# A third pair of PSUM banks after three norms, level chains on other slots, and 37 low parts on VectorE instead of GpSimd, in a two-block transformer kernel

## What is computed

```python
# block 1
h = rms_norm(x, mix_pre_g);  q, k, v, f, qh, i, g = split(h @ w_in)
o_da = differential_attention(q, k, v)      # 8 heads, causal softmax
o_hg = hgrn2(f, qh, i, g)                   # 8 heads, decayed linear attention:
#   attn[t,s] = sum_c q[t,c] k[s,c] exp(b[t,c] - b[s,c]),  b = cumsum(log f)
x = x + rms_norm(concat(o_da, o_hg) @ w_out)
h = rms_norm(x, cross_pre_g);  qx = h @ w_cq;  kx, vx = split(rms_norm(mem) @ w_ckv)
x = x + rms_norm(softmax(qx kx^T) vx @ w_co)
x = x + rms_norm((silu(gate) * up) @ w_ffn_out)      # hidden width 5632
# block 2
h = rms_norm(x);  p, q, k, v, g_lr, r, gates = split(h @ w_in_2)
# pooling branch, gated linear attention with the same kind of decay, gates, w_out_2, second FFN
```

## Time and profile before

| what | value |
|---|---|
| median of 3 runs | 2911.67 us |
| the profiled execution | 2912.26 us, of which the span is 2910.4 us |
| PE busy | 2847.8 us, 98% of the span |
| DVE busy | 1753.1 us, 60% |
| ACT busy | 1397.6 us, 48% |
| POOL busy | 194.7 us, 7% |
| granted TensorE clock, mean | 0.993 of full speed |

### The profile page before, as it was taken

The page is one execution under the profiler, slowest core; times in us unless marked ns, Lnnn a source line. Parts: engine busy times, 40 slices in busy tenths (PEclk is TensorE's granted clock), DMA queues, the critical chain, the costliest instruction groups (busy, mean ns, idle before and its releaser), DMA issues.

```text
span 2910.4 us, 37252 instructions
## 1 busy us (share of the span) xinstructions
PE 2847.8 (98%) x15236; PEld 2431.7 (84%) x15236; DVE 1753.1 (60%) x1936; ACT 1397.6 (48%) x1705; POOL 194.7 (7%) x109
## 2 busy tenths in 40 slices
PE   8998999999999999999999999999999999999998
PEld 6887888778888888887788887888878888888886
DVE  5668765666645555556468654666566654565555
ACT  5555444564444443445545544454454444443443
POOL 1022210110000000002222000000010000000001
PEclk9999999999999999999999999999999999999999
DMA  7554445455665656555555465665656566556654
GB/s 245 160 159 151 118 157 189 160 166 182 196 196 179 195 181 202 179 185 166 162 166 167 145 189 165 186 191 187 195 175 194 182 198 191 182 178 205 186 183 159
DMA packets 432090, 520.56 MB, mean 179 GB/s; under 512 B 18032, under 2 KB 346144, under 8 KB 431280
## 3 DMA queue, kind: packets, MB, share of 16 engines
q1 hardware_dynamic: 430304, 510.52, 56.6%
q0 software_dynamic: 1328, 7.42, 0.7%
q10 hardware_dynamic: 288, 0.24, 0.1%
HBM read 516.01 MB, written 2.11 MB: 178 GB/s over the span
## 4 chain that ended last, share of the span: by engine, by line
PE 89%; DVE 5%; DMA 2%; ACT 2%; issue 1%; POOL 0%; SPq 0%; DVEq 0%; ACTq 0%
PE PS L460 88%; DVE RL L1366 1%; DVE AR L1366 1%; DMA RAW<-in_w_in 1%; DVE X L1372 1%; ACT RH L923 1%; DMA RAW<-in_w_ffn_out 1%; DMA RAW<-in_w_ffn_down 1%; PE PS L463 1%; ACT SP L923 1%; DVE A_HL L1372 0%; ACT AR L923 0%; POOL ST L1970 0%; DVE AR L1369 0%; POOL RL L1947 0%
## 5 line engine op out<-in xcount | busy, mean ns | idle before, releaser
L1366 DVE TENSOR_TENSOR RL<-RAW,RH 128x1024 fp32r<-128x1024 f32 x917 | 1126.2, 1240 | 899.8 <-ACT RH L923 895.6
L923 ACT ACTIVATE RH<-RAW 128x1024 fp32r<-128x1024 f32 (+1 forms) x961 | 1004.1, 1057 | 1003.7 <-PE PS L460 616.0
L460 PE MATMUL PS<-A_HL,RH 128*128 128x512 f32 (+1 forms) x3280 | 1165.5, 399 | 8.7 <-DVE AR L1366 3.2
L460 PE MATMUL PS<-A_HL,RL 128*128 128x256 f32 (+1 forms) x3280 | 920.7, 281 | 0.0
L460 PEld LDWEIGHTS PS<-A_HL,RH 128*128 128x128 f32 (+1 forms) x3280 | 616.4, 188 | 159.0 <-issue 4.7
L460 PE MATMUL PS<-B_HL,RH 128*128 128x512 f32 x1856 | 656.6, 399 | 0.5 <-DVE B_HL L1372 0.5
L460 PEld LDWEIGHTS PS<-A_HL,RL 128*128 128x128 f32 (+1 forms) x3280 | 620.2, 189 | 1.4 <-issue 0.7
L460 PE MATMUL PS<-RH,A_HL 128*128 128x512 f32 x1728 | 539.1, 391 | 0.1
L460 PE MATMUL PS<-B_HL,RL 128*128 128x256 f32 x1856 | 520.8, 281 | 0.0
L460 PEld LDWEIGHTS PS<-B_HL,RH 128*128 128x128 f32 x1856 | 348.7, 188 | 87.1 <-DVE B_HL L1372 0.7
L460 PEld LDWEIGHTS PS<-RH,A_HL 128*128 128x128 f32 x1728 | 325.1, 188 | 69.0 <-DVE RL L1366 1.0
(11 more groups left out here) (105 smaller groups left out, 1069.4 us busy)
## 6 DMA issues: line engine op xcount, KB each, us to landing
RAW<-in_w_in SPq DMA_DIRECT2D x288, 512.0 KB, 3.8
RAW<-in_w_ffn_in SPq DMA_DIRECT2D x176, 512.0 KB, 4.5
RAW<-in_w_ffn_out SPq DMA_DIRECT2D x88, 512.0 KB, 4.7
RAW<-in_w_ffn_gate SPq DMA_DIRECT2D x88, 512.0 KB, 4.5
RAW<-in_w_ffn_up SPq DMA_DIRECT2D x88, 512.0 KB, 4.5
RAW<-in_w_ffn_down SPq DMA_DIRECT2D x88, 512.0 KB, 4.7
RAW<-in_w_out SPq DMA_DIRECT2D x64, 512.0 KB, 4.6
RAW<-in_w_branch_b SPq DMA_DIRECT2D x32, 512.0 KB, 4.4
```

What stands on the lines that cost most here:

```text
L460: return g.matmul(o, l, r, start=start, stop=stop, skip_group_check=True)
L923: return g.activation(o, i, f, bias=bias, scale=scale, accum_out=accum)
L1366: return g.tensor_tensor(o, a, b, f)
```

## The change

Six things change. (1) Three passes, the first pass of k0, ckv1, and LR, go to the pair [4, 5] (`THIRD`) instead of taking the next of the two pairs; they are the passes that follow a normed group. Every later pass outside the FFNs' own rotation shifts with that, and cross attention moves to the banks 6, 7 and the pair of cq's first pass (`CROSS_BANKS`). (2) The 37 low parts of the set `shared` (every third slot of f, qh, i, g0, g1, K, Q, P) are made by VectorE; 7 stay on GpSimd. (3) Chains 0 and 2 start 2 slots later against chains 1 and 3, and chains 2 and 3 half a slot later as a whole. (4) `DA_NORM` moves from slots 75 and 80 to 88 and 91. (5) A head's product with the values, and the copy behind it, come half a slot later. (6) The steps of cross attention come half a slot later, with the one on VectorE at +3 moved to +3.5 and those on TensorE and ScalarE at +4.5 moved to +5.

```diff
@@ build
+        THIRD = [("k0", 0), ("ckv1", 0), ("LR", 0)]
@@ one_pass
             passes.setdefault(name, []).append(ids)
+            key = (name, len(passes[name]) - 1)
+            if key in THIRD:
+                unit[key] = [4, 5]
+                return
             b = 2 * (turns[0] % units)
             turns[0] = b // 2 + 1
-            unit[name, len(passes[name]) - 1] = [b, b + 1]
+            unit[key] = [b, b + 1]
@@
-        shared = [n for n in groups if n[0] in "fiKQP" or n[:2] in ("qh", "g0", "g1")]
-        on_pool = {i for n in shared for i in groups[n] if i % 3 == 0}
-        on_pool |= {i for n in ("q0", "cq", "co0", "co1", "Fg0", "K0", "Hg0") for i in groups[n][1:2]}
+        on_pool = {i for n in ("q0", "cq", "co0", "co1", "Fg0", "K0", "Hg0") for i in groups[n][1:2]}
@@
+        CROSS_BANKS = [6, 7] + unit["cq", 0]
@@
-        DA_NORM = [first("qh1") + 3, first("i0")]
-        HG_START = [first("f1") + 2, first("i0") - 1]
+        DA_NORM = [first("i1"), first("i1") + 3]
+        HG_START = [first("f1") + 2, first("i0") - 0.5]
@@
-            plan, at, done = level_plan(HG_LEVELS[part], HG_START[j] + (3, 0)[part], 6, 2, (0, 0, 0), hg_at)
+            plan, at, done = level_plan(HG_LEVELS[part], HG_START[j] + (5, 0)[part], 6, 2, (0, 0, 0), hg_at)
@@ head_task on TensorE
-                yield HEAD[h] + 7.5
+                yield HEAD[h] + 8
@@ head_task on VectorE
-                yield HEAD[h] + 8
+                yield HEAD[h] + 8.5
@@ cross_task on TensorE (PS[:, 4 + h becomes PS[:, CROSS_BANKS[h] on all engines)
-                yield CROSS + 0.5
+                yield CROSS + 1
...
-                yield CROSS + 4.5
+                yield CROSS + 5
```

More of the change, by code:

```diff
@@ L754, in cross_task @@
                     for blk in range(2):
-                        t = mm(PS[:, 4 + h, blk * T:blk * T + T], by_head(QX)[:, h, blk * P:blk * P + P], by_head(KT)[:, h, :],
+                        t = mm(PS[:, CROSS_BANKS[h], blk * T:blk * T + T], by_head(QX)[:, h, blk * P:blk * P + P], by_head(KT)[:, h, :],
                                blk == 0, True)
                     t.then_inc(s_c_m, 1)
-                yield CROSS + 4.5
+                yield CROSS + 5
                 for h in range(4):
@@ L762, in cross_task @@
                         for blk in range(2):
-                            t = turn(PS[:, 4 + h, kb * T + blk * P:kb * T + blk * P + P], PX[:, 2 * h + blk, kb * P:kb * P + P])
+                            t = turn(PS[:, CROSS_BANKS[h], kb * T + blk * P:kb * T + blk * P + P], PX[:, 2 * h + blk, kb * P:kb * P + P])
                     t.then_inc(s_c_m, 1)
@@ L879, in tensor @@
                     for kb in range(2):
-                        t = mm(PS[:, 4 + i, c * T:c * T + T], VX[:, kb, h * P:h * P + P],
+                        t = mm(PS[:, CROSS_BANKS[i], c * T:c * T + T], VX[:, kb, h * P:h * P + P],
                                PT[:, 512 * h + kb * T:512 * h + kb * T + T], c == 0 and kb == 0, kb == 1)
@@ L1098, in cross_task @@
                 nm, total = stat("cross_max", 8), stat("cross_sum", 8)
-                yield CROSS + 1.5
+                yield CROSS + 2
                 for h in range(4):
@@ L1103, in cross_task @@
                         n = 2 * h + blk
-                        t = act(PX[:, n, :], PS[:, 4 + h, blk * T:blk * T + T], ACT.Exp, bias=nm[:, n:n + 1],
+                        t = act(PX[:, n, :], PS[:, CROSS_BANKS[h], blk * T:blk * T + T], ACT.Exp, bias=nm[:, n:n + 1],
                                 accum=total[:, n:n + 1])
                     t.then_inc(s_c_a, 1)
-                yield CROSS + 4.5
+                yield CROSS + 5
                 for h in range(4):
                     g.wait_ge(s_c_m, 5 + h)
-                    act(PT[:, 512 * h:512 * h + 512], PS[:, 4 + h, :]).then_inc(s_c_a, 1)
+                    act(PT[:, 512 * h:512 * h + 512], PS[:, CROSS_BANKS[h], :]).then_inc(s_c_a, 1)
             def decay_task():
@@ L1287, in scalar @@
                 g.wait_ge(s_c_m, 9 + i)
-                act(BH[:, 2 * i:2 * i + 2, :], PS[:, 4 + i, :].rearrange("p (c t) -> p c t", c=2)).then_inc(s_c_a, 1)
+                act(BH[:, 2 * i:2 * i + 2, :], PS[:, CROSS_BANKS[i], :].rearrange("p (c t) -> p c t", c=2)).then_inc(s_c_a, 1)
             tokens(1, 1, 2)
@@ L1638, in cross_task @@
                 nm, total, inv = stat("cross_max", 8), stat("cross_sum", 8), stat("cross_inv", 8)
-                yield CROSS + 1
+                yield CROSS + 1.5
                 for h in range(4):
                     g.wait_ge(s_c_m, h + 1)
-                    red(nm[:, 2 * h:2 * h + 2], PS[:, 4 + h, :].rearrange("p (b k) -> p b k", b=2), ALU.max,
+                    red(nm[:, 2 * h:2 * h + 2], PS[:, CROSS_BANKS[h], :].rearrange("p (b k) -> p b k", b=2), ALU.max,
                         negate=True).then_inc(s_c_v, 1)
-                yield CROSS + 3
+                yield CROSS + 3.5
                 g.wait_ge(s_c_a, 4)
@@ L1871, in vector @@
                 g.wait_ge(s_c_a, 9 + i)
-                tt(BL[:, 2 * i:2 * i + 2, :], PS[:, 4 + i, :].rearrange("p (c t) -> p c t", c=2),
+                tt(BL[:, 2 * i:2 * i + 2, :], PS[:, CROSS_BANKS[i], :].rearrange("p (c t) -> p c t", c=2),
                    BH[:, 2 * i:2 * i + 2, :].bitcast(F32), ALU.subtract).then_inc(s_c_v, 1)
```

## The result

The kernel after takes 2879.54 us (median of 4 runs, 2878.86 to 2881.43), the kernel before 2912.56 us on the same chip (4 runs, 2910.64 to 2915.98). The ratio is 0.9883, 95% interval 0.9868 to 0.9898: 33 us less. The forecast was 2887. The profiled run of after is its longest, 2881.43 us with a span of 2879.6.

The account below looks back on a forecast made before the run. TensorE, busy 98% of the span, was taken as the bound, so only its idle 62.6 us or low-clock time could be won. 7.8 + 11.3 + 3.2 + 4.4 - 1.5 = 25.2 us off 2912.3 gave 2887, range 2878 to 2901.

Parts of the forecast that it names:

- the forecast scenario: Whole kernel, rival 1: all terms come true, 2887 us, own range 2881 to 2892; chance 0.55.
- rival 3: All dips go, no new wait, later stages gain 2 us: 2880 us, range 2874 to 2881; chance 0.10.
- Banks, 7.8: Start of k0, ckv1 and LR: a third pair of banks removes TensorE's idle of 1.78, 2.84 and 3.15 us.
- Chains, 11.3: Level chains: chain 3's first-product wait falls from 7.30 to 1.2 us; waits of 0.57, 1.72 and 2.92 go.
- Heads, 3.2: Heads: four TensorE waits for ScalarE's copy of the turned scores, 3.2 us in sum, go; largest 2.04.
- Clock, 4.4: Three half-clock stretches, 283.6 to 379.2 us, may go with the chains' waits: bounds 0 and 6.6, 4.4 taken.
- New waits, -1.5: Slots 88 to 91: VectorE's 16.8 us of work against TensorE's about 17; 1.5 us allowed, bounds -0.5 and 8.
- 37 low parts, plus 5 us of VectorE's time and no cost to TensorE: First mixer: 21 low parts add 24 us to VectorE, 19 us of blocked time goes; net plus 5 us.
- Rival 2: Fuller VectorE keeps the level chains late, waits and dips stay: 2899 us, range 2892 to 2905; chance 0.23.
- Rival 5: VectorE's queue falls over two slots behind, slots 84 to 99; ten products wait 3.1 us each: 2920 us; chance 0.04.

Follow-up runs that it names:

- old spacing: After, with chains 0 and 2 back at 3 slots against chains 1 and 3 in place of 5: 2915.94 us, ratio 1.0007 to the kernel before.
- heads alone: The kernel before with only the heads' products and the copies behind them half a slot later: 2912.71 us, ratio 0.9997.
- chains with low parts: The kernel before with the new chain and head-norm slots and all 37 low parts on VectorE: 2891.54 us, ratio 0.9928.
- norms, low parts: Two runs on after: head norms back at their old slots, 2882.53 us; the 37 low parts back on GpSimd, 2888.38 us.
- the banks alone: The kernel before with only the third pair of banks, cross attention's new banks and its later slots: 2903.77 us, ratio 0.9964.
- the chains another half slot later: After, with chains 2 and 3 another half slot later, starting at i0: 2878.71 us, ratio 0.9888 to the kernel before.
- the old heads: After, with the heads' products and the copies behind them back at their old half slots: 2879.32 us, ratio 0.9882 to the kernel before.
- the chains alone: The kernel before with only the level chains' and head norms' slots moved: 2906.20 us, ratio 0.9972.
- all chains on their old slots: After, with all four chains back on their old slots (spacing 3, chains 2 and 3 starting at i0 - 1): 2900.66 us, ratio 0.9955 to the kernel before.
- the old cross slots: After, with cross attention's steps back at their old half slots: 2879.19 us.

## Why the prediction was right, point by point

The result, 2879.54, lies in the predicted range of 2878 to 2901 and 7.5 us below the forecast of 2887. It is outside the forecast scenario's own range, 2881 to 2892: what came true is rival 3 (2880; all dips go, no new wait), to which the prediction gave a chance of 0.10. Its 2 us from later stages did not show: behind slot 168 the lead grows only at LR's wait and at one stretch at half clock, told below. Every sign that the prediction named is there: no idle at k0, ckv1 and LR; 0.74 us at chain 3's first product (foretold near 1); no wait of 1.7 or 2.9; no matmul that waits for `SP` (the 0.2 us are a transpose's); scans of 1.2; no half clock in the mixer; idle time 40.4 (about 42).

- **Banks, 7.8.** Right: the three waits are gone, the table's leads around them add 2.4, 3.7 and 2.6 us (to slot 449), and alone the part brought 9.8 without a later wait.
- **Chains, 11.3.** Right in mechanism and size: of 12.5 us waited, 0.74 is left, so 11.8. The kernel with old spacing shows that the cause named for the waits of 1.72 and 2.92, a product too close behind the copy that it needs, was the right one and can cost more than the prediction thought. One reading is off by 0.2 us: TensorE stood from 280.0 (287.34 - 7.30), not from 279.8.
- **Heads, 3.2.** In the profile 3.3 (heads alone), 2.0 taken out of after. In the medians it doesn't show.
- **Clock, 4.4.** Mis-sized: it was the full 6.6, the upper bound. The doubt whether the waits cause the dips is answered for the mixer as far as runs go: with the waits gone they go (after, chains with low parts), and a wait put back brings one back at its place (norms, low parts). It is no strict rule: head 6's wait of 2.04 us in the kernel before has no dip behind it, and that of 2.02 with the banks alone has one.
- **New waits, -1.5.** Mis-sized: none in the mixer. VectorE's load between slots 88 and 91 was summed rightly: these operations take 16.5 us from start to start, against 16.8.
- **37 low parts, plus 5 us of VectorE's time and no cost to TensorE.** This is the weakest step of its reasoning. The net load was about +0.7 us, not +5: 21 low parts more at 1.13 us from start to start are 24 us, and the busy time rose by 0.7, so 23 us of stretched operation went, where the prediction had counted 19. The other 4 lie in the operations that read `ST`, which it left out. And TensorE's side was not nothing: with GpSimd's low parts back the kernel is 8.8 us slower by the medians, and the profile puts this in the mixer. The prediction looked for the part's worth in a mean load and gave it none of its own (2.2 us inside the chains' term, head 6's wait inside the heads'); the worth lies in where a blocked operation stands, ahead of a multiplication that a product waits for. The sum was right for the whole change, since its terms took away every wait at once; read as prices of single parts it would have misled, for 11 of the 33 us exist only when chains and low parts are both made.
- **Second order.** 3.4 us went back in the FFN at slots 176 to 240. Some 2.4 came from the start (0.7) and from a stretch at half clock (1.7) of the kernel before at 1416.8 that the profile of after lacks. Neither is work of the change: that stretch stands in the profiles with the chains another half slot later and with the old heads (at 1387 in each), which are as quick as after.

Rival 2 (VectorE, fuller, keeps the chains late) failed although VectorE's share of the mixer rose from 73% to 80%: its work took no longer, and the copies came in time. Rival 5 named about 3 us of wait at product after product from slot 84 on. The old spacing with the new start shows such waits, at 2915.9. The place was foretold well; that the price (2920) came near is in part luck. Rival 5 took ten waits of 3.1 us, 31 in all, with the half clock as before; measured were seven waits of 20.9 us in all, with 34 us at half clock. The cause is also only in part the one it named, since in the largest of these waits VectorE stood still for another engine. That the change stays clear of it is the doing of the two slots more between chains 0 and 1, and between 2 and 3.

The Trainium skill, "SBUF — State Buffer", section "SBUF: two separate sides", has VectorE and GpSimd share a port pair as an exclusive lock. The runs agree: VectorE's 128x512 operation ends 0.55 us behind GpSimd's low part, 2.91 us against 0.69. By this rule such a stall is not a share of bandwidth but what is left of the other engine's operation, here 2.2 us at one place, which is why the mean misleads.

## What to carry to other kernels

Price work on GpSimd beside VectorE not by the mean of the stretched operations but by the place: look up which of VectorE's operations starts while GpSimd runs, and how many instructions stand between it and what TensorE waits for. When two engines follow one written order, leave the partner's answer some slack. Two slots were enough here; with the question and the answer at the same slot TensorE waited 1.3 to 4 us at six of eight products, and ahead of the three longest VectorE itself stood waiting for ScalarE, which waited for TensorE; the clock behind the waits cost almost as much again. One slot was not tried. Two edits that work on the same queue are to be priced together, since each may bring little until the other has been made.

## What the runs showed of the hardware

- **Short waits and the clock.** In the profiles of the chains alone and of after with GpSimd's low parts, TensorE waited nine times for 1.3 to 1.9 us in the mixer, and in 7 of the 9 a stretch of 3.4 us at half clock followed. None came behind the heads' shorter waits in these two profiles, of 0.4 us (three times) and 0.6, and elsewhere longer ones stayed without one: k0's 1.78 and ckv1's 2.84 us in the kernel before. With the waits of 3.3 to 4.0 us (old spacing) came stretches of 3.4 to 6.8 us, and behind one of 2.9 us (all chains on their old slots) one of 10.2. So where a stretch comes, an estimate from these lengths is that the wait costs itself and half the stretch, 1.7 to 5.1 us, more. A wait is not the only thing that goes ahead of such a stretch: the profiles have single ones at 557 to 605 us and at 1387 to 1422 us too, in other places from kernel to kernel, and for those no cause was looked for.
- **Two paces at the same clock.** In the first FFN's groups at slots 192 to 240 the matmuls of 512 columns start 230 ns after each other in the kernel before, and 236 ns in after, at a granted clock of 1.00 in both, with the same instructions. Elsewhere most FFN groups are at 236 in both, and slots 569 to 600, ahead of the second FFN, at 230 in both. The second FFN's groups at slots 713 to 760 ran at 230 with the heads alone, at 231.7 with the old cross slots, and at 236 in before and after. 6 ns on 512 matmuls are 3.1 us, so this may be a good part of the spread between runs; each kernel has one profile, which can't show it. What sets the pace is open; no experiment here was aimed at it.
